# A low-rank gate as a narrow product, and the linear-attention products by pairs between dense chunks

## The reference, cut to what matters

```python
h = rmsnorm_2(x, norm1_g)                      # x: the first block's output after its final norm
proj = h @ w_in                                # 1024 -> 4112 columns
q, k, v, r, a_low, u_pool, gate_gla, gate_pool = jnp.split(proj, split_idx, axis=-1)
                                               # 256, 256, 512, 512, 16, 512, 1024, 1024 columns
log_a = log_sigmoid(a_low @ w_alpha_up + b_alpha) / 16.0
o = gla_mix(q, k, v, log_a)                    # 4 heads, key width 64, value width 128, chunks of 64 tokens
o = head_rmsnorm(o, gla_norm_g) * silu(r)
y_gla = o @ w_gla_branch
y_pool = pool_mix(u_pool, pool_w, pool_scale) @ w_pool_branch   # trailing means over 2, 4, 8, 16 tokens
merged = sigmoid(gate_gla) * y_gla + sigmoid(gate_pool) * y_pool
x = x + merged @ w_out                         # then a mixture of 32 experts, and a final norm
```

## Time and profile before

| | |
|---|---|
| median of 3 runs | 1377.55 us (1374.88 to 1379.21) |
| the profiled execution | 1376.56 us, of which 1374.7 us between its first and last instruction |
| mean granted TensorE clock | 0.974 of full speed |
| PE busy | 1275.1 us (93%) |
| DVE, ACT, POOL busy | 611.8 us (45%), 463.2 us (34%), 529.9 us (39%) |
| second in-projection on PE | from 738.9 us to 982.2 us |
| last stage, the experts | from about 1108 us to the end; the DMA engines 0.90 busy |

### The profile page before, as it was taken

How to read it: one execution, slowest core, us unless ns; L and a number is a source line. 1 busy time by engine, 2 the same in 40 slices (tenths; PEclk the granted TensorE clock), 3 DMA queues, 4 the chain that set the end, 5 groups by cost and what they waited for, 6 DMA issues and landing times.

```text
span 1374.7 us, 17033 instructions
## 1 busy us (share of the span) xinstructions
PE 1275.1 (93%) x5934; PEld 939.9 (68%) x5934; DVE 611.8 (45%) x1132; ACT 463.2 (34%) x769; POOL 529.9 (39%) x685
## 2 busy tenths in 40 slices
PE   5999999999999999999999997999999679998784
PEld 4767777788888888888887686777888533333331
DVE  4758767626434222222257548336252432222115
ACT  5656544444434132232344342145222200000002
POOL 2644332335555545555455645223553011111100
PEclk9999999999999999999999999899999779999998
DMA  5432212123333333333363334112329579999984
GB/s 185 110 77 59 65 47 62 47 62 92 107 92 91 108 92 101 89 102 97 92 205 93 93 78 107 31 47 66 109 79 401 218 280 421 424 425 424 425 356 186
DMA packets 210901, 214.56 MB, mean 156 GB/s; under 512 B 30363, under 2 KB 192861, under 8 KB 198164
## 3 DMA queue, kind: packets, MB, share of 16 engines
q1 hardware_dynamic: 201760, 203.48, 43.6%
q0 software_dynamic: 4752, 8.10, 1.6%
q10 hardware_dynamic: 4324, 2.12, 0.5%
HBM read 206.11 MB, written 16.78 MB: 162 GB/s over the span
## 4 chain that ended last, share of the span: by engine, by line
issue 41%; POOL 30%; PE 24%; DVE 2%; ACT 2%; DMA 1%; POOLq 0%; DVEq 0%; ACTq 0%
POOL wlo L578 30%; PE bank L1931 9%; PE bank L1948 5%; PE bank L1630 2%; PE bank L1632 2%; PE bank L1631 2%; DMA x_rows<-x_out 1%; PE side L1660 1%; ACT hid L963 1%; DVE hid L1483 1%; PE side L1632 1%; PE side L1631 1%; PE side L1630 1%; PE side L1859 0%; ACT hidT L966 0%
## 5 line engine op out<-in xcount | busy, mean ns | idle before, releaser
L578 POOL TENSOR_TENSOR wlo<-raw,whi 128x256 fp32r<-128x256 f32 x648 | 496.2, 798 | 569.9 <-ACT whi L679 569.8
L1631 PE MATMUL bank<-actB_lo,whi 128*128 128x512 f32 x616 | 240.9, 391 | 0.0
L1630 PE MATMUL bank<-actB_hi,whi 128*128 128x512 f32 x584 | 231.6, 397 | 6.0 <-POOL wlo L578 4.6
L1632 PE MATMUL bank<-actB_hi,wlo 128*128 128x512 f32 x584 | 228.7, 392 | 0.0
L679 ACT ACTIVATE whi<-raw 128x1024 fp32r<-128x1024 f32 x162 | 169.8, 1051 | 155.8 <-PE bank L1632 128.0
L1630 PE MATMUL bank<-actA_hi,whi 128*128 128x512 f32 x400 | 156.6, 391 | 0.5 <-POOL wlo L578 0.5
L1632 PE MATMUL bank<-actA_hi,wlo 128*128 128x512 f32 x400 | 155.7, 389 | 0.0
L1631 PE MATMUL bank<-actA_lo,whi 128*128 128x512 f32 x400 | 155.6, 389 | 0.0
L1931 PE MATMUL bank<-gu,xeT 128*64 128x512 f32 x528 | 127.0, 618 | 12.5 <-issue 11.0
L1631 PEld LDWEIGHTS bank<-actB_lo,whi 128*128 128x128 f32 x616 | 116.5, 189 | 24.6 <-issue 0.7
L1630 PEld LDWEIGHTS bank<-actB_hi,whi 128*128 128x128 f32 x584 | 110.5, 189 | 31.4 <-POOL wlo L578 3.9
(11 more groups left out here) (364 smaller groups left out, 1644.3 us busy)
## 6 DMA issues: line engine op xcount, KB each, us to landing
gu<-in_w_exp_gate SPq DMA_DIRECT2D x33, 1024.0 KB, 18.8
gu<-in_w_exp_up SPq DMA_DIRECT2D x33, 1024.0 KB, 21.9
dn<-in_w_exp_down SPq DMA_DIRECT2D x33, 1024.0 KB, 24.2
raw<-in_w_in SPq DMA_DIRECT2D x58, 512.0 KB, 3.9
raw<-in_w_up SPq DMA_DIRECT2D x32, 512.0 KB, 3.9
raw<-in_w_down SPq DMA_DIRECT2D x32, 512.0 KB, 3.9
raw<-in_w_out SPq DMA_DIRECT2D x16, 512.0 KB, 4.0
raw<-in_w_in SPq DMA_DIRECT2D x16, 256.0 KB, 3.2
```

What stands on the lines that cost most here:

```text
L578: ins = nc.gpsimd.tensor_tensor(wlo[:, slot, at], raw[:, slot, at], whi[:, slot, at].bitcast(F32), ALU.subtract)
L1630: mm(b[:, :], w_hi, hi[:, k, :], start=first, stop=False)
L1631: mm(b[:, :], w_hi, lo[:, k, :], start=False, stop=False)
L1632: ins = mm(b[:, :], w_lo, hi[:, k, :], start=False, stop=last)
```

## The change

1. **Low-rank gate.** The dense chunk +0 goes (161 chunks are left). Instead PE runs 8 plain matmuls with 32 columns of weights each (`wlow`) straight on `xT`, four to the four groups of 32 output rows of one `side` bank, the other four added on top. ACT copies the bank to `alow`, and the job `z` adds the four groups up by itself, since `wal` now holds `w_alpha_up` four times, at rows 0, 32, 64 and 96. The norm factor `rs` is multiplied in by DVE after `z` (one more operation for each of the two). `z` now comes after chunk +1, ahead of `sum2` and `sum3`.
2. **Increments, scores, heads.** An increment is now four products of 64 rows by 64 columns by 128 in place of two of 64 by 128 by 256, and two increments (even and odd: lower and upper 64 rows of the keys) alternate. Scores and heads are made two heads at a time, one on the lower 64 rows and one on the upper, alternating. DVE's state update acts on 128 partitions and so is 13 operations instead of 28.
3. **Places.** Increments stand between chunks +13, +14, +15 and +16, scores after +16, heads 0 and 1 after +18, heads 2 and 3 after +20. The pooling products stand after +22 and the last sum of squares, as the last jobs of the table. The trailing means of the fourth window move behind the take of chunk +17, and each mean is one operation shorter in its long part.
4. **ACT.** The first parts of chunks +4 and +5 move ahead of and between the first guesses; one table load is left there instead of two.
5. **SP.** The small loads (`wal`, `pw`, the router's weights) and the zeroing of `y2_rows` move from the end of the first block's MLP into its four quarters.

```diff
+            b = open_job("alow")
+            pe.wait_ge(S("low_scaled"), 1)
+            for half in range(2):
+                pe.wait_ge(S("x1_made"), 4 * half + 4)
+                for q in range(4):
+                    ins = mm(b[32 * q:32 * (q + 1), :], wlow[:, 4 * half + q, :], xT[:, 4 * half + q, :], start=half == 0, stop=half == 1)
+            close_job(ins)
-            chunks(C_IN2, 1, *inB)
-            total("sum2", ssum[:, :], S("sum_added"), 3 * NK)
-            total("sum3", ssum2[:, :], S("sum_added"), 3 * NK)
-            chunks(C_IN2 + 1, 4, *inB)
+            chunks(C_IN2 + 1, 1, *inB)
+            wait_freed(pe, "alow")
...
+            total("sum2", ssum[:, :], S("sum_added"), 3 * NK)
+            total("sum3", ssum2[:, :], S("sum_added"), 3 * NK)
+            chunks(C_IN2 + 2, 3, *inB)
...
+            def increments(*pair):
+                banks = [open_job(("inc", n)) for n in pair]
                 for j in range(2):
-                    ins = mm(b[:, 256 * j:256 * (j + 1)], kend_tok[rows, n // 2, j * P:(j + 1) * P],
-                             gv_tok[rows, n // 2, 256 * j:256 * (j + 1)], start=True, stop=True)
-                close_job(ins)
+                    for e in range(2):
+                        h = 2 * j + e
+                        for b, n in zip(banks, pair):
+                            rows = slice(CHUNK * (n % 2), CHUNK * (n % 2 + 1))
+                            ins = mm(b[HD * e:HD * (e + 1), j * DV:(j + 1) * DV],
+                                     kend_tok[rows, n // 2, j * P + HD * e:j * P + HD * (e + 1)],
+                                     gv_tok[rows, n // 2, h * DV:(h + 1) * DV], start=True, stop=True)
...
+            def heads_of(j):
+                banks = [open_job(("o", 2 * j + e)) for e in range(2)]
+                for t in range(NT):
+                    cols = slice(t * P, (t + 1) * P)
+                    for e, b in enumerate(banks):
+                        h = 2 * j + e
+                        mm(b[:, cols], gv_tok[:, t, h * DV:(h + 1) * DV], scT[:, h, cols], start=True, stop=False)
+                    for n in range(2 * t, 2 * t + 2):
+                        if n:
+                            at_ = slice(n * CHUNK, (n + 1) * CHUNK)
+                            for e, b in enumerate(banks):
+                                rows = slice(HD * e, HD * (e + 1))
+                                ins = mm(b[:, at_], gst[rows, j, n, :], qdec[rows, j, at_], start=False, stop=n % 2 == 1)
...
+            chunks(C_IN2 + 13, 1, *inB)
+            wait_freed(pe, ("kend_tok", 1))
+            increments(0, 1)
+            chunks(C_IN2 + 14, 1, *inB)
+            increments(2, 3)
+            chunks(C_IN2 + 15, 1, *inB)
+            increments(4, 5)
+            chunks(C_IN2 + 16, 1, *inB)
+            increments(6)
+            for j in range(2):
+                scores_of(j)
+            chunks(C_IN2 + 17, 1, *inB)
+            chunks(C_IN2 + 18, 1, *inB)
+            wait_freed(pe, ("scores", GH - 1))
+            for j in range(2):
+                heads_of(j)
+                for e in range(2):
+                    chunks(C_IN2 + 19 + 2 * j + e, 1, *inB)
+                    total(("o_sum", 2 * j + e), sq[:, e, :], S("o_squares"), 2 * j + e + 1)
             pe.wait_ge(S("diff_made"), 4)
             for g in range(4):
                 close_job(mm(open_job(("pool", g))[:, :], pw[:, g, :], diff[:, g, :], start=True, stop=True))
...
+            chunks(C_IN2 + 23, 10, *inB)
+            wait_freed(pe, ("pool", 3))
```

The job table, which sets which job waits for which:

```diff
+    for h in range(0, GH, 2):
+        for name in ("o", "o_sum"):
+            for e in range(2):
+                jobs.add((name, h + e), "dve")
     for g in range(4):
         jobs.add(("pool", g), "dve")
-    for h in range(GH):
-        jobs.add(("o", h), "dve")
-        jobs.add(("o_sum", h), "dve")
-    for h in range(1, GH):
-        jobs.free_first(("o", h), ("o_sum", h - 1))
```

More of the change, by code:

```diff
@@ L177, in job_table @@
                 jobs.add(("probs_t", s - 1, half), "act")
-    for n in (1, 2, 3):
+    jobs.add("sum1", "dve")
+    jobs.add("alow", "act")
+    for j in range(2):
+        jobs.add(("z", j), "dve")
+    for n in (2, 3):
         jobs.add(f"sum{n}", "dve")
     for j in range(2):
-        jobs.add(("z", j), "dve")
+        jobs.free_first(("z", j), f"sum{2 + j}")
     for h in range(GH):
@@ L890, in _ @@
                 act.wait_ge(S("r_silu"), h + 1)
-            for c in range(C_IN2 + 13, C_IN2 + 17):
-                first_part(c + AHEAD)
             for j in range(2):
@@ L896, in _ @@
                   ACT.Copy).then_inc(side_freed["act"], 1)
+            for c in range(C_IN2 + 13, C_IN2 + 17):
+                first_part(c + AHEAD)
             def gate(c):
@@ L903, in gate @@
                 a(t, t, ACT.Sigmoid).then_inc(S("gate_made"), 1)
-            for c in range(C_IN2 + 17, C_IN2 + 21):
-                gate(c)
             def head_first(h):
@@ L925, in _ @@
                 split_first("branch2", actA_hi, 4 + g, diff[:, g, :], None)
-            for c in range(C_IN2 + 25, C_IN2 + 33):
+            for c in range(C_IN2 + 23, C_IN2 + 33):
                 gate(c)
@@ L1299, in _, with windows @@
             inv = const("inv_count")
-            for g, win in enumerate(WINDOWS):
-                take(C_IN2 + 13 + g, diff[:, g, :])
+            def windows(g):
                 src, step, n = diff[:, g, :], 1, 0
-                while step < win:
+                while step < WINDOWS[g]:
                     dst = pool_t[:, n % 2, :]
@@ new lines, in gate, with head_norm, head @@
+            def gate(c):
+                j = c - C_IN2 - 17
+                take(c, sg2[:, j // NK, j % NK, :])
+            def head_norm(h):
+                refine(side_of(("o_sum", h))[:, :], rs_h[h % 2][:, :], DV, freed=freed)
+                t = o_s[h % 2][:, :]
+                chain(v.scalar_tensor_tensor(t, t, g_gla[:, h:h + 1], rs_h[h % 2][:, :], ALU.mult, ALU.mult))
+                chain(v.tensor_tensor(t, t, rsil[:, h, :], ALU.mult), S("o_normed"))
+            def head(h):
+                wait_job(dve, ("o", h))
+                dve.wait_ge(S("o_squares"), h + 1)
+                chain(v.tensor_copy(o_s[h % 2][:, :], side_of(("o", h))[:, :]), freed)
@@ L1324, in _, with head_second @@
+            def head_second(h):
+                second("branch2", actA_hi, actA_lo, h, o_s[h % 2][:, :], None)
+            for g in range(3):
+                take(C_IN2 + 13 + g, diff[:, g, :])
+                state(2 * g)
+                state(2 * g + 1)
+                windows(g)
+            take(C_IN2 + 16, diff[:, 3, :])
+            state(6)
             for h in range(GH):
@@ L1328, in _ @@
                                       const("pair_causal").unsqueeze(1).broadcast_to([P, NT, P]), ALU.mult), freed)
+            gate(C_IN2 + 17)
+            windows(3)
+            gate(C_IN2 + 18)
+            head(0)
+            head(1)
+            gate(C_IN2 + 19)
+            head_norm(0)
+            gate(C_IN2 + 20)
+            head_norm(1)
+            head_second(0)
+            head(2)
+            head_second(1)
+            head(3)
+            gate(C_IN2 + 21)
+            head_norm(2)
+            gate(C_IN2 + 22)
+            head_norm(3)
+            head_second(2)
+            head_second(3)
             for g in range(4):
@@ L1815, in _ @@
-            for h in range(GH):
-                b = open_job(("scores", h))
-                rows = slice(HD * (h % 2), HD * (h % 2 + 1))
+                    for e in range(2):
+                        h = 2 * j + e
[4 more added lines that the diff above has]
+                                     gv_tok[rows, n // 2, h * DV:(h + 1) * DV], start=True, stop=True)
+                            if (j, e) == (1, 1):
+                                close_job(ins)
```

178 lines of the change are left out of this document (79 added, 99 removed).

## The result

| | before | after |
|---|---|---|
| median (runs) | 1377.95 us (4: 1374.88 to 1379.21) | 1351.65 us (4: 1348.63 to 1352.34) |
| ratio to before, 95% interval | | 0.9815 [0.9801, 0.9829] |
| profiled execution | 1376.56 us | 1348.63 us |
| the stage: last matmul of the MLP to the branch projection | 243.7 us | 217.6 us |

The account below looks back on a forecast made before the run. PE sets the pace up to about 1108 us, then expert weight loads; PE's savings arrive in full. Terms 4.1 + 5.0 + 2.8 + 10.4 + 2.9 + 4.7 + 2.2 - 7.1 = 25.0 us, forecast 1352, range 1347 to 1358.

Parts of the forecast that it names:

- Gate: Low-rank gate: 16 records four abreast replace a dense chunk and its waits, 7.3 us before; 4.1 us saved.
- First stall: PE's wait for wlo near 760 and the lower clock after it go through ACT's new order; 5.0 us saved.
- Covered waits: Waits before value transposes, before increments and for a later wlo get dense work in front; 2.8 us saved.
- Increments: State increments between chunks, 56 records in 3.5 us in place of 13.9 us; 10.4 us saved.
- Scores: Scores in alternating halves, 2.2 us plus about 1.1 of waiting in place of 6.2; 2.9 us saved.
- Heads: Heads in pairs at 5.0 us each, 14.7 us before; 4.7 saved, with one loss of 1.8 left in.
- Pooling products: Last jobs: 2.2 us saved at full clock, 7.1 lost waiting for the last head's norm chain and at lower clock.
- SP: Small loads moved into the MLP's quarters: 0 us, bound 3 us lost.
- The rival without overlap: Row halves and column groups don't overlap in gate, increments, scores and heads: 16 us saved, 1360 us; chance 0.12.
- The one without a pooling wait: ACT and DVE run through the heads without lag, clock stays up: 30 us saved, 1347 us; chance 0.12.
- given back later: Expert stage set by something that doesn't move with PE: 0 to 4 us saved, 1375 us; chance 0.04.
- the lower clock didn't spread: Rival: small products between single chunks keep the clock low, ten chunks lose 44 us, 1395 us; chance 0.04.

Follow-up runs that it names:

- experiment 2: Changed kernel, but ACT makes the first parts of chunks +4 and +5 behind both first guesses again; 1351.30 us, ratio 0.9817.
- Experiment 1: Changed kernel, but all eight gate products go to one group of 32 output rows, one after another; 1354.61 us, ratio 0.9843.
- experiment 3: Kernel before the change, with only ACT's new order of first parts ahead of and between the guesses; 1374.40 us, ratio 0.9970.
- Experiment 4: Changed kernel, but all seven paired increments in one block after chunk +16, DVE making all trailing means before the states; 1359.72 us, ratio 0.9874.
- experiment 8: Changed kernel, but chunks +23 to +25 go ahead of the pooling products, with two ACT first parts earlier; 1339.09 us, ratio 0.9730.
- Experiment 6: Changed kernel, but ACT's first part of chunk +25 goes behind its last guess, so POOL is idle during head 2's norm; 1352.92 us, ratio 0.9815.
- experiment 5: Changed kernel, but products of paired row halves issued one half after the other in increments, scores and heads; 1352.87 us, ratio 0.9816.

## Why the prediction was right, and where not

Measured terms, the predicted ones in brackets:

- **Gate: 4.7 (4.1).** 2.6 us as worked out. Of the 0.7 us wait before `z` at most 0.15 is there: ScalarE's copy ends at 746.99 and `z` starts at 747.04, 5.77 us after the chunk's first matmul; in experiment 2, with the copy earlier, it is 5.62. Experiment 1 shows the four groups.
- **First stall: 5.0 (5.0).** The size is right, the step's cause only in part. "The cause is ACT: its first parts stand behind both guesses" is true of the kernel before (experiment 3), but in the changed kernel 4 of the 5 us go without the new order (experiment 2). The step treated ScalarE's order as the one remedy and overlooked that the gate and `z`, now ahead of the unprepared chunk, fill most of the wait. (Its times for the bank of chunk +1 don't add up: 751 and 13.6 are 764.6, not 763. DVE had taken the chunk at 764.6 and PE needed the bank at 766.91, so nothing hung on it.)
- **Covered waits: 2.8 (2.8).** None of the three is left.
- **Increments: 10.8 (10.4).** 3 x 0.82 and 0.59 for the seventh, 3.05 us for 3.5 worked out. Experiment 4 puts 8 to 9 us of this and the next line together on the new places.
- **Scores: 3.1 (2.9).** 3.09 us with a wait of 0.84; 1.1 was given.
- **Heads: 7.1 (4.7).** A pair is 4.60, not 5.0, which makes 5.5. And of the clock loss of 1.8 that I left in, 1.6 isn't there: the second pair starts 12.80 us after the first has ended, and two chunks and two sums are 12.6.
- **Pooling products: 2.2 saved, 11.1 lost (7.1).** This is the step that was mis-sized. From 886.91 to 901.5, where chunk +23 would have had to start at full clock, are 14.6 us; 3.44 are the products. The serial chain was the right mechanism. Its length was E + 36.8 for E + 32.9 (E, the end of chunk +19, is 862.32): norms of heads 0 and 2 took 5.9 us in place of 4.4 (3.1 together), because POOL worked beside them, and the other 0.8 are hand-overs between the engines, 0.03 to 0.27 us each. All four norms of the old trace take 4.4, and POOL is idle beside each. I took the duration of an operation as its own, where it depends on a neighbour. The old trace did show this elsewhere, in the same operation of two refinements, with POOL idle and with POOL at work (from 758.66 on):

```profile
752.59 0.69 DVE L1012 SCALAR_TENSOR_TENSOR rsf<-ssum,rsf 128x512 f32<-128x512 f32 x1
...
759.98 1.10 DVE L1012 SCALAR_TENSOR_TENSOR rs<-ssum,rs 128x512 f32<-128x512 f32 x1
```

- **SP: 0 (0).** The MLP, where the small loads now stand, ends as early as before (738.31 for 738.52).

They add up to 24.6 us, and the stage is 26.2 shorter. The distances between the chunks' first matmuls say where the other 1.6 us lie: 0.7 from the gate to the end of the first stall and of `z` (10.4 saved there for the 9.7 above), 0.5 at the covered waits, 0.3 at the heads. A chunk behind a wait or behind small products starts one or a few tenths late, and the brackets don't hold that. The gate, the increments, the scores and the heads saved 3.6 us more than predicted, and the pooling products lost 4.0 more. That the forecast landed within a microsecond is luck: these two cancelled. Either alone would have left it inside its range (about 1348 or 1356).

The rival without overlap fell with the gate's first row; experiment 1 prices its largest part. The one without a pooling wait fell with the 8.96 us, and experiment 8 shows what it would have been: 11.1 us in the stage, 12.6 in the time (7.1 + 1.8 was the upper price given). The gain wasn't given back later. And the lower clock didn't spread: with small products between chunks it stayed at 1.00 from 818.60 to 841.10.

The drain between kinds of product, which the Trainium skill names in TensorEngine Tiling (Array Packing), Key Properties, shows here as 0.2 us at most: from one pair of increments to the next are 6.26 us, of which the pair takes 0.60 up to the next chunk's start and the chunk 5.44. The 0.22 that are left are the size that I read from the heads. But a chunk behind transposes of full height, with no change of tiling, is late by 0.12 too (795.78 to 801.34 is 5.56), so the drain's own part may be as little as 0.1.

## What to carry over

Small products that feed another engine cost little between dense chunks and much in a block, since the block waits for that engine and the clock then falls too. When work is taken out of a block, ask of each piece which bank it needs and who frees it last: the last piece needs the same cover as the first, and three chunks of cover for the pooling products were worth nearly half as much as the whole change (11.1 us of the stage for 26.2). Take the length of a serial chain from the place where its neighbours will be busy, and look at what an engine does in its idle time, such as a table load, before moving the work in front of it.

## What the runs showed of the hardware

- **DVE beside POOL.** DVE's 128x512 operations with two SBUF inputs take 1.10 us while POOL works and 0.69 otherwise; POOL's take 1.08, and 0.70 alone (four in 2.82 us at 858.93). Experiment 6 switches the slowing off. The Trainium skill, SBUF — State Buffer, Who interferes with whom, says that such an instruction contends with a GpSimd instruction that reads SBUF, which agrees. It also calls the contention an exclusive lock; by strict turns an operation of each would need 1.4 us together, and the rows show 1.1, so for this pair the measurement stands against it. An operation with one of its two inputs in PSUM keeps 0.69 beside POOL (`ssum<-side,rsf` at 755.12, with POOL at work from 752.44 to 756.38).
- **Four column groups of 32** ran 16 records of 512 columns in 2.06 us, and in 6.99 in one group.
- **What the lower clock costs after a wait varies.** After the same 9.0 us wait, the ten chunks from +23 on took 55.7 us in one profile of the changed kernel and 57.2 in another (54.4 at full clock), with the stage otherwise equal to 0.1 us. All of it lies in chunk +23: 6.7 and 8.2 us, and 6.8 to 7.8 in experiments 1, 2, 4 and 5, for 5.44 at full clock. That is part of the scatter of the times.
- **A lower clock after two short waits.** In experiment 3 PE idled for 1.39 and 0.95 us with three matmuls between, and ran at the lower level (1.2 GHz) afterwards: the granted clock from 747 to 751 us is 0.57. With 1.38 and 0.48 it stayed at the upper one, 1.00. There is one profile of each, so that the half microsecond made the difference is not shown.
